# First norm deferred past the u and z projections, constants loaded on two queues

## The reference, cut to what matters

```python
def rms_norm(x, g):
    y = x * rsqrt(mean(x * x, axis=-1) + 1e-6)
    return y * g

def ssm_layer(x, ...):                       # 512 prompt tokens + 8 samples, d = 1024
    h = rms_norm(x, norm_pre)
    u, z = split(h @ w_in, 2)                # 2048 channels each
    y, hr, hi = s5_scan(u, ...)              # per group of 16 channels, 64 states
    y = y + d_skip * u
    ga, gb = split(gelu(y) @ w_glu + b_glu, 2)
    y = ga * sigmoid(gb) * silu(z)
    return x + rms_norm(y @ w_out, norm_post), hr, hi
```

## Time and profile before

| | us |
|---|---|
| median of 3 runs (1543.17 to 1546.32) | 1545.5 |
| the profiled execution's own time | 1544.77 |
| its span, first to last instruction | 1543.0 |
| TensorE products busy | 1365.5 |
| VectorE busy | 634.1 |
| ScalarE busy | 510.3 |
| GpSimd busy | 522.9 |

### The profile page before, as it was taken

How to read it: one execution, slowest core, us unless ns; L and a number is a source line. 1 busy time by engine, 2 the same in 40 slices (tenths; PEclk the granted TensorE clock), 3 DMA queues, 4 the chain that set the end, 5 groups by cost and what they waited for, 6 DMA issues and landing times. The chain is left out here.

```text
span 1543.0 us, 29855 instructions
## 1 busy us (share of the span) xinstructions
PE 1365.5 (88%) x12197; PEld 1290.5 (84%) x12197; DVE 634.1 (41%) x1010; ACT 510.3 (33%) x889; POOL 522.9 (34%) x310
## 2 busy tenths in 40 slices
PE   5588888978988999999997996799889999999893
PEld 3578878977988999999997995799878887889693
DVE  5866648996921221221220005561234333443314
ACT  4223332414542222222221123232345544545221
POOL 0312222330014344344342331133356555554130
PEclk9789999998999999999999998899999999999897
DMA  5466884431123333333332231134756666563311
GB/s 128 74 128 128 140 118 103 126 111 48 48 71 97 109 92 105 109 94 104 109 99 64 86 92 40 43 86 149 222 181 193 226 193 222 178 219 99 95 54 56
DMA packets 271635, 178.84 MB, mean 116 GB/s; under 512 B 64848, under 2 KB 260136, under 8 KB 271040
## 3 DMA queue, kind: packets, MB, share of 16 engines
q1 hardware_dynamic: 270912, 144.18, 35.7%
q10 hardware_dynamic: 640, 33.49, 6.0%
HBM read 157.36 MB, written 53.77 MB: 137 GB/s over the span
## 5 line engine op out<-in xcount | busy, mean ns | idle before, releaser
L109 POOL TENSOR_TENSOR w_lo<-raw,w_hi 128x1024 fp32r<-128x1024 f32 x168 | 409.0, 2436 | 816.8 <-ACT w_hi L104 609.6
L161 PE MATMUL acc<-act_hi,w_hi 128*128 128x256 f32 x1728 | 353.9, 286 | 30.4 <-POOL w_lo L109 24.0
L161 PE MATMUL acc<-act_lo,w_hi 128*128 128x256 f32 x1728 | 351.8, 285 | 0.0
L161 PE MATMUL acc<-act_hi,w_lo 128*128 128x256 f32 x1728 | 351.3, 285 | 0.0
L161 PEld LDWEIGHTS acc<-act_hi,w_hi 128*128 128x128 f32 x1728 | 271.8, 191 | 32.9 <-issue 26.4
L104 ACT ACTIVATE w_hi<-raw 128x1024 fp32r<-128x1024 f32 x156 | 164.8, 1057 | 343.0 <-PE acc L161 289.6
L161 PEld LDWEIGHTS acc<-act_lo,w_hi 128*128 128x128 f32 x1728 | 271.6, 191 | 0.0
L161 PEld LDWEIGHTS acc<-act_hi,w_lo 128*128 128x128 f32 x1728 | 271.4, 190 | 0.0
L1277 DVE SCALAR_TENSOR_TENSOR sig<-acc,vec,sig 128x520 f32<-128x520 f32 x16 | 12.2, 760 | 293.4 <-PE acc L161 293.4
L1821 PE MATMUL acc<-act_hi,w_hi 128*128 128x256 f32 (+1 forms) x512 | 112.9, 302 | 8.9 <-ACTq L2076 8.7
L1821 PE MATMUL acc<-act_lo,w_hi 128*128 128x256 f32 (+1 forms) x512 | 105.1, 287 | 0.0
(11 more groups left out here) (298 smaller groups left out, 2062.6 us busy)
## 6 DMA issues: line engine op xcount, KB each, us to landing
raw<-a_w_glu SPq DMA_DIRECT2D x64, 512.0 KB, 4.0
s_kv<-cache_kv ACTq DMA_DIRECT2D x8, 4088.0 KB, 16.3
raw<-a_w_in SPq DMA_DIRECT2D x32, 512.0 KB, 4.3
raw<-b_w_in SPq DMA_DIRECT2D x32, 512.0 KB, 4.5
raw<-a_w_out SPq DMA_DIRECT2D x16, 512.0 KB, 3.6
raw<-w_kv SPq DMA_DIRECT2D x16, 512.0 KB, 3.9
k_rows<-cache_kv SPq DMA_DIRECT2D x32, 256.0 KB, 7.4
v_rows<-cache_kv SPq DMA_DIRECT2D x16, 512.0 KB, 6.6
```

What stands on the lines that cost most here:

```text
L109: pool.tensor_tensor(self.mem.wl[s][:, :, :], self.mem.raw[s][:, :, :], self.mem.wh[s][:, :, :].bitcast(F32), ALU.subtract).then_inc(self. ...
L161: ins = nc.tensor.matmul(mem.acc[a][:, 256 + lo:256 + hi], w[s][:, k, :], x[:, k0 + k, lo:hi], start=first and k == 0 and i == 0, stop=las ...
```

## The change

The norm's high and low parts are now those of x times the gain alone, and the first two tiles of u are computed before the sum of squares. 1/rms is kept for all stages in `x_rstd` and applied to u when it leaves PSUM (now by VectorE, `scale_u`) and to z in the gated unit. z is stored raw, and SiLU becomes z * sigmoid(z) there. The seven vectors and the imaginary half of C are loaded on ScalarE's queue, B ahead of C on the sync queue. x lands in another place, so that its high parts can be written while it is transposed; two GELU buffers move.

```diff
@@ setup, sync queue
-            (the seven loads of vrow)
             dn.load_first(sp)
-            (32 loads of crow, 2 of h0row)
             (4 loads of Bt)
+            load_c(sp, 0, range(8))
+            (2 loads of h0row)
@@ setup, TensorE
             ins.then_inc(l_full, 1)
+            pe.wait_ge(v_in, 16 * 7)
+            nc.tensor.transpose(aux[3][:, 0:NVEC], vrow[:, :], ...).then_inc(v_full, 1)
 ...
+            pe.wait_ge(x_moved, DT)
+            dn.first_tiles(pe, mem.acth, mem.actl, lambda k: pe.wait_ge(nm.act_lo, k + 1))
+            pe.wait_ge(free, 9)
             for f in range(DT):
                 nm.add(pe, f, f % 2, f == 0, f == DT - 1)
-            pe.wait_ge(x_moved, DT)
-            dn.first_tiles(pe, mem.acth, mem.actl, lambda k: pe.wait_ge(nm.act_lo, k + 1))
             pe.wait_ge(c_in, 16 * 32)
@@ setup, ScalarE
+            (the seven loads of vrow)
             act.wait_ge(l_in, 48)
 ...
             act.activation(dw[:, 5:7, :], dw[:, 3:5, :], ACT.Sin).then_inc(a_out, 1)
+            load_c(act, 1, range(4))
+            def high(f):
+                act.wait_ge(x_moved, f + 1)
+                act.activation(mem.acth[:, f, :], mem.xT[:, f, :], ACT.Copy,
+                               scale=mem.vec[:, V_APRE + f:V_APRE + f + 1]).then_inc(nm.act_hi, 1)
+            act.wait_ge(free, 9)
             for f in range(DT):
                 act.wait_ge(full, f + 1)
                 act.activation(mem.xT[:, f, :], acc[f % 2][:, 0:TOK], ACT.Copy).then_inc(x_moved, 1)
+                if f >= 1:
+                    high(f - 1)
+                if f == 4:
+                    dn.split_hi_first(act)
+            high(DT - 1)
             for f in range(DT):
                 nm.square(act, f, f % 2, mem.xT[:, f, :])
+            load_c(act, 1, range(4, 8))
             nm.take_root(act)
-            dn.split_hi_first(act)
-            nm.apply_hi(act, 0)
@@ setup, VectorE
+            v.wait_ge(v_full, 1)
+            v.tensor_copy(mem.vec[:, :], aux[3][:, 0:NVEC]).then_inc(free, 1)
             v.wait_ge(l_full, 1)
 ...
+            for f in range(DT):
+                v.wait_ge(nm.act_hi, f + 1)
+                v.scalar_tensor_tensor(mem.actl[:, f, :], mem.xT[:, f, :], mem.vec[:, V_APRE + f:V_APRE + f + 1],
+                                       mem.acth[:, f, :].bitcast(F32), ALU.mult, ALU.subtract).then_inc(nm.act_lo, 1)
             for j in range(L):        # cb
 ...
             nm.invert(v)
-            nm.apply(v, V_APRE, 0)
@@ states, ScalarE
             def batch(b, q, h, first=False):
                 for i in range(2):
-                    copy_u(2 * b - 2 + i, i, b - 1)
                     dn.split_hi(act, 2 * b + i, i, b)
@@ states, VectorE
+            def scale_u(m, i, b):
+                dn.wait_tile(v, m)
+                v.wait_ge(u_stored, 32 * b + 32)
+                v.tensor_tensor(ust[i][:, :], columns(mem.acc[i]), mem.x_rstd[:, :], ALU.mult).then_inc(u_copied, 1)
+                v.wait_ge(u_copied, m + 1)
+                v.sem_inc(dn.acc_free[i], 1)
 ...
                 build(b, tab[q])
+                if not (first and b == 0):
+                    for i in range(2):
+                        scale_u(2 * b + i, i, b)
                 copy_k(b)
@@ gate_and_scan, ScalarE
-                act.activation(zst[i][:, :], columns(mem.acc[i]), ACT.Silu).then_inc(z_copied, 1)
+                act.activation(zst[i][:, :], columns(mem.acc[i]), ACT.Copy).then_inc(z_copied, 1)
@@ glu, ScalarE
+                act.wait_ge(z_scaled, i + 1)
+                act.activation(sz[s][:, :], zt[s][:, :], ACT.Sigmoid).then_inc(z_sig, 1)
                 dn.split_hi(act, 4 * i + 3, 1, 2 * i + 1)
@@ glu, VectorE
+                v.wait_ge(z_in[s], 16 * h + 16)
+                v.tensor_tensor(zt[s][:, :], zt[s][:, :], mem.x_rstd[:, :], ALU.mult).then_inc(z_scaled, 1)
                 dn.wait_tile(v, 2 * i + 1)
 ...
-                v.sem_inc(gated, 1)
-                v.wait_ge(z_in[s], 16 * h + 16)
+                v.tensor_tensor(sg[s][:, :], sg[s][:, :], zt[s][:, :], ALU.mult).then_inc(gated, 1)
 ...
-                v.tensor_tensor(yt[s][:, :], sg[s][:, :], zt[s][:, :], ALU.mult).then_inc(prod, 1)
+                v.tensor_tensor(yt[s][:, :], sg[s][:, :], sz[s][:, :], ALU.mult).then_inc(prod, 1)
```

More of the change, by code:

```diff
@@ L249, in plan @@
     mem.rest = o
+    mem.x_rstd, _ = mem.at("x_rstd", [P, TOK], (mem.end - mem.base) // 32 * 32 - TOK * 4)
     return mem
@@ L294, in setup, with load_c @@
         dve = sem("dve_chain")
+        v_full = sem("vec_transposed")
         dt_ready, l_full, x_moved = sem("dt_ready"), sem("lam_transposed"), sem("x_moved")
         a_in, a_out = sem("act_ask"), sem("act_done")
+        def load_c(eng, ri, blocks_of):
+            c = ten[("a_c_re", "a_c_im")[ri]][0, :, :, :].rearrange("(c e) o p -> e c o p", e=2)
+            for t in blocks_of:
+                for e in range(2):
+                    eng.dma_start(crow[:, ri, t, 64 * e:64 * e + 64], c[e, 8 * t:8 * t + 8, :, :]).then_inc(c_in, 16)
         block = ctx.enter_context(nc.Block())
@@ L347, in _ @@
             ins.then_inc(l_full, 1)
+            pe.wait_ge(v_in, 16 * 7)
+            nc.tensor.transpose(aux[3][:, 0:NVEC], vrow[:, :], mem.ident[0:NVEC, 0:NVEC]).then_inc(v_full, 1)
             pe.wait_ge(x_in, 16 * 9)
@@ L379, in _ @@
         def _(act):
+            at = 0
+            for name in ("a_norm_pre", "a_norm_post", "kv_norm", "b_norm_pre", "b_norm_post", "a_d", "a_b_glu"):
+                v = ten[name] if name == "kv_norm" else ten[name][0, :]
+                n = v.shape[0] // P
+                act.dma_start(vrow[at:at + n, :], v.rearrange("(f p) -> f p", p=P)).then_inc(v_in, 16)
+                at += n
             act.wait_ge(l_in, 48)
@@ L483, in _ @@
             for ri in range(2):
-                v.wait_ge(full, 14 + ri)
+                v.wait_ge(full, 13 + ri)
                 v.tensor_copy(mem.XH[:, ri, :, C_FIRST:C_LAST], aux[2 + ri][:, :].rearrange("p (s c) -> p c s", s=NS))
@@ L738, in _ @@
             paired(act, 2, NB, batch)
-            for i in range(2):
-                copy_u(WT - 2 + i, i, NB - 1)
             nxt.split_hi_first(act, dn, WT)
@@ L796, in batch @@
                     couple(mem, v, mem.a8, b - 1, 1, 2, terms, total, paired_up, b - 1)
+            for i in range(2):
+                scale_u(i, i, 0)
             for b in range(2):
@@ L1039, in outputs @@
             l.append(t)
-    yt.append(mem.at("y_gelu0", [P, TOK], o)[0])
-    yt.append(mem.at("y_gelu1", [P, TOK], mem.actl_at + (WT - 1) * TOK * 4)[0])
+    for s in range(2):
+        yt.append(mem.at(f"y_gelu{s}", [P, TOK], mem.actl_at + (WT - 2 + s) * TOK * 4)[0])
     o = mem.ring_at
@@ L1203, in glu @@
     mem.glu_end = o
[L1204 removed]
+    sg, zt, yt, sz = [], [], [], []
     for s in range(2):
[L1206 removed]
+        for name, l in (("sig", sg), ("z_in", zt), ("y_f32", yt), ("z_sig", sz)):
             t, o = mem.at(f"{name}{s}", [P, TOK], o)
```

49 lines of the change are left out of this document (14 added, 35 removed).

## The result

The changed kernel takes 1550.9 us (median of 8 runs, 1549.2 to 1554.7) against 1545.3 for the kernel before in the same comparison: 5.6 us more, a ratio of 1.0049 [1.0035, 1.0062]. Repeated beside other kernels it gave 1.0066 [1.0044, 1.0088]. It is slower, a little more than the 0.2% that can be told from no change. The forecast was 1543.7 and "same". Three executions among the comparisons of this study took over 3,300 us and are left out of the ratios.

The account below looks back on a forecast made before the run. It took barrier-separated stages as bounded by their last instructions, with room only in setup and states. Setup +0.7, states -3.3 and gated unit +0.8 gave -1.8 us: 1543.7 on the median, "same", 8-in-10 range 1540 to 1562.

Parts of the forecast that it names:

- the 0.78 us: States stage, each batch: ScalarE's copy of u and the gap behind it vanish; five batches count, 3.9 us gained.
- The term of -3.3 us: States stage: net gain of 3.3 us from moving u's copies from ScalarE to VectorE, bounds 1.0 and 4.5.
- The step that failed: States stage: u's later store has several us of slack except in the last batch, where 0.6 us is charged.
- Setup: Setup stage: products begin 15.8 us earlier but the tail grows; 0.7 us lost, from 62.2 to 62.7 at the end.
- The four terms: Setup's tail: 7.5 us on sums, 5.1 on issues, 2.1 on the root, 3.4 on the reciprocal.
- the 15.8 us: Setup: TensorE's first product begins at 28.2 instead of 43.97 us, a head start that the tail spends.
- The five us of C issues: Setup's tail: ScalarE issues the other eight C loads behind the last square, ahead of the root, 5.1 us.
- The gated unit: Gated unit: one more product and gap behind the last tile, first tile may wait; 0.8 us lost, bounds 0.7 and 2.5.
- First rival: Setup: B issues on the sync queue hold up ScalarE's C issues, x starts 18 us late; 1561.7 us, chance 0.33.
- Second rival: Setup's tail: second C loads cost no time before the root, 5.1 us shorter; 1538.6 us, chance 0.11.
- Third rival: States stage: VectorE's two products and GpSimd-lengthened build steps overrun 3.5 us free, the 3.9 us gain goes; 1547.6, chance 0.08.

Follow-up runs that it names:

- batch 1 was mended: Changed kernel with batch 1's two u tiles scaled by VectorE before the table build, not behind it: 1548.1 us, 1.0035 to the kernel before.
- the second run: Changed kernel with the second eight C loads issued on ScalarE's queue ahead of the squares, not behind them: 1548.6 us, 1.0034 to the kernel before.

## Why the prediction was wrong

**What bounds the states stage** was the first mistake. The prediction read the earlier trace rows by the busy times of the engines and left the DMA share out. A round of the sync queue (gather, weight loads, chunk store, stores of u) did not get shorter than some 19.4 us over four rounds in any kernel with whole chunk stores, and the batches of before were 19.4 already. With half the chunk store gone the last four of the changed kernel's were 18.7: about the 0.78 us less that the prediction had promised the compute engines, though no run shows that it is the same time. So 0.78 us off ScalarE's part of each batch could gain next to nothing: the compute engines only came to wait for the queue (ScalarE 41.5 us for weights). Whether before was held by this floor or by its own compute, just as long, isn't settled, as the half chunk store was not tried in it. Its rows speak for the floor: in its last four rounds the second store of u landed 3.1 to 4.1 us after its issue and 0.6 to 1.1 behind the chunk store, where such a store lands in 2.1 with the chunk store out of its way. By these rows an earlier copy of u would have waited there; no run tried it. The term of -3.3 us was right in its mechanism, TensorE's waits for ScalarE fell from 10.4 to 3.9 us once batch 1 was mended, and worth at most 0.7.

**The step that failed** is the sentence "The later store of u has several us of slack except in the last batch". The slack was read from a batch in the middle, where the build ends before u leaves TensorE. In batch 1 it is the other way round: the build starts late, GpSimd's low parts stretch it, and TensorE already waited for it before the change (3.6 us for the block-diagonal table). There the store moved by 11.9 us and the gather by 10.9. A delay can only be made good in rounds with slack: before, the gaps between gathers were 23.7, 26.2, 20.3 and then 19.4 to 19.5; after, 33.3, then 20.8, 20.9, 20.7, 19.9, 19.7, 19.2. Of 9.7 us lost in the first, 5.4 came back in the second, the next four lost 2.6 more, the last gave 0.3 back: 6.6 us late at the last gather, seen from the first. With the start, 7.8 late on the clock. Halving the chunk store gave the rounds slack and the lateness went.

**Setup** was off by a size only: +1.7 (+2.3 in the repeat) against +0.7, within its bounds of -1.5 and +2.5. The working held to 0.6 us up to the root, and to 0.3 at the reciprocal's end. Of the 1.0 us missed, 0.6 is TensorE at the lower clock, which cost 1.1 and which the text had named ("up to 1.5 us more") and taken at 0.5. Its 62.7 for the barrier was the end of the last copy; the barrier stands 0.3 behind that in both kernels. The four terms that it says spend the 15.8 us add up to 18.1, as the issues lie partly beside the last square and its sum. The five us of C issues were the term to attack, and the second run took 3.4 of them.

**The gated unit** was right: 0.5 to 0.6 measured for 0.8, and all of it behind the last tile. The product's 0.70 us and its gap are there; VectorE and ScalarE took the fifteen others beside TensorE.

**First rival, the queues hold each other up: refuted.** Bt loads on the sync queue in the changed kernel: ns shortest/median/longest, first and last start.

```profile
L321 SPq DMA_DIRECT2D Bt<-a_b_re x2: 4696/5809/6922, 9.5 to 14.2; - x2
```

Two issues took 11.7 us (9.5 to 21.2) on the sync queue, and ScalarE's eight took 5.19 us in just that time, 0.60 us each, 0.74 the longest. In the other direction it is open: the same two issues took 4.09 us before, and whether ScalarE's issues or the loads queued ahead of them stretched them, no run separates; nothing waited for B so early. The Trainium skill, "Perfetto Trace Analysis", section "DMA Instruction - HWDGE (DVE, Sync)", has the descriptor generator shared and locked for each DMA; by that the eight would have waited. No issue here shows it, and the measurement decides. The time nevertheless fell into the range that this rival had opened upward (1540 to 1562), for another reason.

**Second rival, the head start survives: refuted** as such, the root was at 53.83. It was made true by hand in the second run. **Third rival, VectorE as the bound: partly right.** It named the stretched build step, and that a gain would go. It looked at batches 3 to 7, where it did not happen, and followed TensorE's wait for the table, not the sync queue's for u.

**Sum:** +1.7 for the setup, +5.6 for the states, +0.5 behind the sigmoid, and +1.4 in the two stages between that no run tied to the change: 9.2 us between the two profiles, of which the medians show 5.6. The other 3.6 us are the spread of single executions: the profiled one is the second slowest of the eight. Where it arises stays open.

## What to carry to other kernels

Before a faster engine is booked as a gain, look at the DMA share and at the issue times of one repeating transfer: if these repeat with the batch and the pieces between them don't change from batch to batch, the batch belongs to the queue. Read the slack of a moved instruction in every batch that has a different order around it, the first and second above all, and ask of a late transfer whether the rounds behind it have room to catch up. Put work that only feeds a store ahead of a long build on the same engine, and issue DMAs from a compute engine where it has nothing on the critical path.

## What the runs showed that was not expected

- Moving a large store to a second hardware queue did not make room. The store of u landed in 2.1 us for 8.8, the gathers in 8.2 for 2.7, the weight loads in 7.8 for 4.7, the chunk store in 11.3 for 11.7; the stage was 178.9 us, as in the repeat of the changed kernel.
- The chunk store, 584 KB, needs 11.3 to 11.7 us to land; half of it 7.9 us. Over two batches, with gathers, weight loads and stores of u, the engines moved 138 GB/s on average at an 84% busy share, while the fastest fortieth of that window reached 347 GB/s. 9,610 of its 14,194 packets are under 512 B. A busy DMA engine says little about bytes; the kind of transfer counts. The Trainium skill, "DMA: Bandwidth & Descriptors", section "Specifications", wants at least 512 B a transfer for full rate; these rows agree in direction, and no run here changed the packet size.
- Pauses of TensorE at the end of the setup cost 1.1 us through the clock, and taking the late issues out of them gave none of it back: with the issues early TensorE still idled 4.4 us behind the reciprocal and 8 transposes took 1.97 us at a clock of 0.50; with the reciprocal last it idled 0.4 us and they took 1.26 at 1.00.
